# Attention's values on two column tiles, sums of probabilities on GpSimd, maxima written straight into the queries

## The reference, cut to what matters

```
s = (einsum("bqhd,bkhd->bhqk", q_nope, k_nope) + einsum("bqhr,bkr->bhqk", q_rope, k_rope)) * SM_SCALE
s = where(allowed, s, finfo(float32).min)
p = softmax(s, axis=-1)
out = einsum("bhqk,bkhd->bqhd", p, v)
```

## Time and profile before

| | us |
|---|---|
| median of three runs | 1343.7 (1342.97 to 1345.61) |
| the profiled execution, its own time | 1344.39 |
| span of its instructions | 1342.6 |
| PE busy in it | 1312.1 (98%) |
| DVE, ACT, POOL busy | 891.2, 502.8, 57.3 |
| the eight heads of attention | 434.0 to 587.3 |

### The profile page before, as it was taken

One profiled execution on the slowest core, in us unless ns is written; L12 is line 12 of the kernel. 1 busy time (PEld: TensorE's weight loads), 2 busy tenths in 40 slices (PEclk: granted clock), 3 DMA queues, 4 the chain that ended last, 5 costly groups with the idle time before them and its releaser, 6 DMA issues.

```text
span 1342.6 us, 22926 instructions
## 1 busy us (share of the span) xinstructions
PE 1312.1 (98%) x9288; PEld 1245.7 (93%) x9288; DVE 891.2 (66%) x1391; ACT 502.8 (37%) x833; POOL 57.3 (4%) x59
## 2 busy tenths in 40 slices
PE   6999999999999999999999999999999999999997
PEld 4799999999997677789999999999999999999997
DVE  6699988382655567777885545656456569877743
ACT  5622221234301444346643333333333336444532
POOL 0200000000013122200000000000000000000000
PEclk9899999999999999999999999999999999999999
DMA  9445534711213332030232232331323276455441
GB/s 352 142 142 149 160 116 114 279 37 31 91 30 68 110 78 45 1 100 13 68 101 88 63 110 97 119 103 58 108 88 119 88 275 235 118 178 160 163 138 79
DMA packets 132759, 154.75 MB, mean 115 GB/s; under 512 B 12065, under 2 KB 99705, under 8 KB 130641
## 3 DMA queue, kind: packets, MB, share of 16 engines
q1 hardware_dynamic: 130080, 152.50, 35.8%
q10 hardware_dynamic: 2608, 1.28, 0.4%
HBM read 115.51 MB, written 30.69 MB: 109 GB/s over the span
## 4 chain that ended last, share of the span: by engine, by line
PE 91%; DVE 5%; ACT 1%; issue 1%; DMA 1%; POOL 0%; SPq 0%; ACTq 0%; DVEq 0%; POOLq 0%
PE PS L1360 30%; PE PS L917 18%; PE PS L1426 12%; PE PS L1456 5%; PE PS L1270 4%; PE PS L1123 4%; PE PS L1503 3%; PE PS L1250 3%; PE PS L1308 2%; PE PS L1011 2%; PE PS L1197 2%; PE PS L1217 1%; PE PS L1151 1%; DVE MX L2432 1%; PE PS L886 1%
## 5 line engine op out<-in xcount | busy, mean ns | idle before, releaser
L1360 PE MATMUL PS<-HBL_T,EH 128*128 128x264 f32 x640 | 169.3, 285 | 0.0
L1360 PE MATMUL PS<-HBH_T,EH 128*128 128x264 f32 x640 | 169.1, 284 | 0.0
L917 PE MATMUL PS<-HH,WH 128*128 128x352 f32 x432 | 139.7, 324 | 1.6 <-DVE CQ L2299 0.8
L917 PE MATMUL PS<-HL,WH 128*128 128x352 f32 x432 | 139.0, 323 | 0.0
L1360 PE MATMUL PS<-HBH_T,EL 128*128 128x264 f32 x640 | 130.4, 285 | 0.0
L1360 PE MATMUL PS<-HBL_B,EH 128*128 128x264 f32 x480 | 127.5, 286 | 0.0
L1360 PE MATMUL PS<-HBH_B,EH 128*128 128x264 f32 x480 | 127.1, 285 | 0.0
L1360 PEld LDWEIGHTS PS<-HBH_T,EH 128*128 128x128 f32 x640 | 120.6, 188 | 0.0
L1360 PEld LDWEIGHTS PS<-HBL_T,EH 128*128 128x128 f32 x640 | 120.3, 188 | 0.0
L1426 PE MATMUL PS<-DTH,DWH 128*128 128x264 f32 x440 | 116.6, 286 | 0.1
L1426 PE MATMUL PS<-DTL,DWH 128*128 128x264 f32 x440 | 116.7, 285 | 0.0
(11 more groups left out here) (346 smaller groups left out, 3166.4 us busy)
## 6 DMA issues: line engine op xcount, KB each, us to landing
ADA<-in_w_ada SPq DMA_DIRECT2D x22, 1024.0 KB, 6.0
DTR<-saved_operands SPq DMA_DIRECT2D x66, 264.0 KB, 2.9
HALF_W<-in_w_gate SPq DMA_DIRECT2D x22, 512.0 KB, 4.0
saved_operands<-UP SPq DMA_DIRECT2D x10, 1056.0 KB, 4.0
RAW<-in_w_in SPq DMA_DIRECT2D x20, 512.0 KB, 6.6
DWR<-in_w_down SPq DMA_DIRECT2D x33, 256.0 KB, 3.2
HALF_W<-in_w_up SPq DMA_DIRECT2D x12, 512.0 KB, 3.7
saved_operands<-TB SPq DMA_DIRECT2D x11, 528.0 KB, 4.8
```

Source lines behind the costliest of these rows:

```text
L917: mm = pe.matmul(PS[:, b + n, 0:CH], w, x[k][:, n * CH:(n + 1) * CH], start=(first and w is weights[0][k] and x is xs[0]), stop=(last and ...
L1360: mm = pe.matmul(PS[:, 2 * s + n, 0:HQ], w, x[:, k, n * HQ:(n + 1) * HQ], start=(first and w is wh and x is xh), stop=(ends and w is wl), ...
```

## The change

Four edits, all in attention:

- `values(h, i)` has 64 stationary columns (the values alone) and becomes two matmuls: the query tiles of even number go to one column tile of PE (PSUM partitions 0 to 63 or 64 to 127), the odd ones to the other; `tile_half` says which. All eight query tiles now fit into bank 4.
- The probabilities of step 0 go to `ACC0`, one buffer per head in turn; `add_probabilities` (POOL) adds those of steps 1 to 7 to it, and `sums(h)` multiplies the total once with the ones, again on two column tiles, in step 0 of the next head (for the last head behind step 8). An exponential waits for the addition two steps back too.
- The maxima go by the same two transfers into `QTH` directly; `MROW` is float32r, so that DVE's copy rounds. `QTM`, `round_maxima` and `max_rounded` are gone; `scores(h, 0)` waits for the transfers.
- `keep_output` copies the values after step 8, the sample's after the next exponential, the sums one step later; `invert_last_sums` waits for all of it.

```diff
+        def row_tiles(ap, first):
+            return ap.rearrange("p (t c) -> p t c", c=P)[:, first::2, :]
+        def tile_half(h, parity):
+            e = (h + parity) % 2
+            return slice(VH * e, VH * (e + 1))
...
 def load_maxima(h):
                 sp.wait_ge(m_kept, h + 1)
-                if h >= 1:
-                    sp.wait_ge(max_rounded, h)
-                sp.dma_start(QTM[PLAIN:CONTRACT, 0:S]..., MROW[0:KD, h % 2, :]).then_inc(max_rows, 16)
-                sp.dma_start(QTM[PLAIN:CONTRACT, S:T], MROW[KD:KD + 1, h % 2, 0:SD]).then_inc(max_rows, 16)
+                if h >= 2:
+                    sp.wait_ge(s_full, STEPS * (h - 1))
+                sp.wait_ge(rounded, 2 * h + 1)
+                row = QTH[h % 2][PLAIN:CONTRACT, :].bitcast(F32)
+                (the same two transfers into row)
...
 def scores(h, i): (i == 0)
-                    pe.wait_ge(max_rounded, h + 1)
+                    pe.wait_ge(max_rows, 32 * (h + 1))
...
 def values(h, i): (i < KD)
-                    for bank, lo, hi, stop in ((4, q0, 512, 3), (5, max(q0, 512), S, KD - 1)):
-                        if lo < hi:
-                            mm = pe.matmul(PS[:, bank, ...], V[:, i, h // 2, VH * (h % 2):VH * (h % 2) + P], PP[...])
+                    for parity in ((0, 1), (1, 0))[i % 2]:
+                        t = i + (i + parity) % 2
+                        if t < KD:
+                            mm = pe.matmul(PS[tile_half(h, parity), 4, P * (t // 2):512], V[:, i, j, P * e:P * e + VH],
+                                           row_tiles(probabilities(h, i), t - i), ...)
+            def sums(h):
+                pe.wait_ge(p_added, (KD - 1) * (h + 1))
+                pe.wait_ge(o_kept, 3 * h + 2)
+                for parity in range(2):
+                    mm = pe.matmul(PS[tile_half(h, parity), 5, :], V[:, 0, 0, VH:2 * VH], row_tiles(ACC0[:, h % 2, :], parity), ...)
...
                         score_maxima(h + 1, (i, 0))
+                    if i == 0 and h >= 1:
+                        sums(h - 1)
                     values(h, i)
...
+            sums(HEADS - 1)
...
 def exponentials(h, i): (0 < i < KD, but for i == 2)
+                    act.wait_ge(p_used, (KD - 1) * h + (i - 1 if i > 1 else 0))
+                    act.wait_ge(p_added, (KD - 1) * h + i - 2)
...
+            def add_probabilities(h, i):
+                n = (KD - 1) * h + i - 1
+                if i == 1:
+                    pool.wait_ge(p_used, n + 1)
+                pool.wait_ge(exp_done, STEPS * h + i + 1)
+                if n >= 1:
+                    pool.wait_ge(p_added, n)
+                pool.tensor_tensor(ACC0[:, h % 2, P * i:], ACC0[:, h % 2, P * i:], PP[:, n % 2, 0:S - P * i], ALU.add)\
+                    .then_inc(p_added, 1)
...
-            round_maxima(0)
-            for h in range(1, HEADS):
-                round_maxima(h)
-                if h + 1 < HEADS:
+            for h in range(HEADS):
+                if 1 <= h < HEADS - 1:
                     round_head(h + 1)
+                for i in range(1, KD):
+                    add_probabilities(h, i)
```

More of the change, by code:

```diff
@@ L1258, in scores, with probabilities @@
                 mm.then_inc(s_full, 1)
+            def probabilities(h, i):
+                return ACC0[:, h % 2, :] if i == 0 else PP[:, (7 * h + i - 1) % 2, 0:S - P * i]
             def values(h, i):
-                n = STEPS * h + i
-                pe.wait_ge(exp_done, n + 1)
+                j, e = divmod(h, 2)
+                pe.wait_ge(exp_done, STEPS * h + i + 1)
                 if i < KD:
-                    q0 = P * i
                     if i == 0 and h >= 1:
-                        pe.wait_ge(o_kept, 3 * h)
-                    for bank, lo, hi, stop in ((4, q0, 512, 3), (5, max(q0, 512), S, KD - 1)):
-                        if lo < hi:
[L1270 to L1277, removed]
+                        pe.wait_ge(o_kept, 3 * h - 2)
+                    for parity in ((0, 1), (1, 0))[i % 2]:
+                        t = i + (i + parity) % 2
+                        if t < KD:
+                            mm = pe.matmul(PS[tile_half(h, parity), 4, P * (t // 2):512], V[:, i, j, P * e:P * e + VH],
+                                           row_tiles(probabilities(h, i), t - i), start=(i == 0), stop=(i == KD - 2 + parity))
+                    mm.then_inc(p_used if i < KD - 1 else o_full, 1)
+                else:
+                    if h >= 1:
+                        pe.wait_ge(o_kept, 3 * h)
@@ L1278, in values @@
                     for m in range(3):
                         _, r = key_tile(KD + m)
[L1280 to L1281 removed]
+                        mm = pe.matmul(PS[:, 5, 0:SD], V[0:r, KD + m, j, VH * e:VH * e + P],
+                                       PSM[0:r, (STEPS * h + i) % 2, SD * m:SD * (m + 1)], start=(m == 0), stop=(m == 2))
@@ L1282, in values @@
                     mm.then_inc(o_full, 1)
+            def sums(h):
+                pe.wait_ge(p_added, (KD - 1) * (h + 1))
+                pe.wait_ge(o_kept, 3 * h + 2)
+                for parity in range(2):
+                    mm = pe.matmul(PS[tile_half(h, parity), 5, :], V[:, 0, 0, VH:2 * VH], row_tiles(ACC0[:, h % 2, :], parity),
+                                   start=True, stop=True)
+                mm.then_inc(o_full, 1)
             pe.wait_ge(ones_kept, 1)
@@ L1750, in exponentials @@
                 act.wait_ge(s_full, n + 1)
-                if i == 0 and h >= 1:
+                if i == 0 and h >= 2:
+                    act.wait_ge(o_full, 3 * h - 3)
+                elif i == 2 and h >= 1:
+                    act.wait_ge(o_full, 3 * h - 2)
+                    act.wait_ge(p_added, (KD - 1) * h)
+                elif 0 < i < KD and (KD - 1) * h + i >= 3:
+                    act.wait_ge(p_used, (KD - 1) * h + (i - 1 if i > 1 else 0))
+                    act.wait_ge(p_added, (KD - 1) * h + i - 2)
+                elif i == KD and h >= 1:
                     act.wait_ge(o_full, 3 * h - 1)
[L1753 to L1756, removed]
                 if i < KD:
                     nq = S - P * i
-                    act.activation(PP[:, n % 2, 0:nq], PS[:, b:b + 2, :].rearrange("p b q -> p (b q)")[:, 0:nq], ACT.Exp,
+                    dst = ACC0[:, h % 2, :] if i == 0 else PP[:, ((KD - 1) * h + i - 1) % 2, 0:nq]
+                    act.activation(dst, PS[:, b:b + 2, :].rearrange("p b q -> p (b q)")[:, 0:nq], ACT.Exp,
                                    scale=SCALE).then_inc(exp_done, 1)
@@ L1774, in keep_output @@
                     act.wait_ge(ao_lo, j - 1)
-                act.activation(OP[j % 2][rows, t], src[rows, :], ACT.Copy)
-                act.activation(SUMS[j % 2][rows, t], src[VH * (1 - e):VH * (2 - e), :], ACT.Copy).then_inc(o_kept, 1)
+                if part == 1:
+                    act.activation(OP[j % 2][rows, S:T], PS[rows, 5, 0:SD], ACT.Copy)
+                    ins = act.activation(SUMS[j % 2][rows, S:T], PS[VH * (1 - e):VH * (2 - e), 5, 0:SD], ACT.Copy)
+                else:
+                    dst, bank = ((OP[j % 2], 4), None, (SUMS[j % 2], 5))[part]
+                    for parity in range(2):
+                        ins = act.activation(row_tiles(dst[rows, 0:S], parity),
+                                             PS[tile_half(h, parity), bank, :].rearrange("p (t c) -> p t c", c=P), ACT.Copy)
+                ins.then_inc(o_kept, 1)
             def round_ao(m):
@@ L1784, in _ @@
             for h in range(HEADS):
-                for i in range(1, 5):
+                for i in range(1, STEPS):
                     exponentials(h, i)
[L1787 to L1790, removed]
+                    if i == 1 and h >= 1:
+                        keep_output(h - 1, 2)
+                    if h == HEADS - 1 and 5 <= i < STEPS - 1:
                         if i == 5:
```

32 lines of the change are left out of this document (11 added, 21 removed).

## The result

The kernel after took **1370.4 us** (median of 4 runs, 1366.85 to 1383.75), the kernel before 1344.2 on the same chip: ratio 1.0216, 95% interval 1.019 to 1.0241. It is slower, as forecast, but by 26 us and not by 12, and the time lies above the range (1342.5 to 1366). Whether it is slower by more than 2% the interval leaves open. The profiled execution took 1371.47 us, its span is 1369.4, 26.8 above the span of before. The mean granted clock of the four runs is 0.984, 0.980, 0.982 and 0.969 for 1366.85, 1369.34, 1371.47 and 1383.75 us: the fastest has the highest and the slowest the lowest.

A forecast was written before the change was run, and what follows sets the result against it. PE, busy for 98% of the span, was taken as the bound. PE's account +0.8, maxima -0.5, POOL against DVE +11.6 and tail +0.2 made +12.1 us on 1343.7: 1356 us, range 1342.5 to 1366.

The forecast's parts named there:

- The account of PE: PE in attention: column tiles save 3.44 us a head, sums add 0.86, switches 2.8; +0.1 a head counted, 0.8 in all.
- The rival that the switch costs nothing: PE's switches between tilings cost nothing with 64 columns and additions stay hidden: 12.8 us saved, 1331 us; chance 0.10.
- the one that the tiles don't run at once: PE's column tiles run one after another, so each head pays sums and switches extra: 1380 us; chance 0.04.
- The maxima: POOL's rounding of the maxima goes; it hid under PE but for 0.5 us, so -0.5 us.
- The additions' own length: POOL's additions take 2.3 ns a column; 3584 columns make 8.2 us, 9.3 with seven waits.
- POOL against DVE: At heads' ends, whichever engine comes second waits for the first's whole instruction, so PE waits: +11.6 us, bounds 0 and 20.
- its marks: Attention: ACT waits for additions, PE for ACT; KTL 2.5 us or more; first maxima product waits for POOL, heads 3 and 5.
- the rival that the casts come late in all heads: DVE wins each contest and POOL's casts come late in all six heads, 1.3 us more each: 1364 us; chance 0.12.
- The sum: Whole kernel: 0.8 - 0.5 + 11.6 + 0.2 (tail) = +12.1 us, added to the median 1343.7: 1356 us.

The follow-up runs named there:

- e10: e9 with the values of steps 4 and 5, and of 6 and 7, next to each other on PE; 1345.84 us, ratio 1.0009 to the kernel before.
- e3: The kernel after without POOL's additions and their waits, the sums replaced by 1; 1344.44 us, ratio 1.0005 to the kernel before.
- e1: The kernel before with only the maxima going directly into the queries; 1342.45 us, ratio 0.9986 to the kernel before.
- e11: The kernel after with DVE made to wait for the additions of steps 4, 5 and 6 before KTL, OP by SUMS and AOH; 1363.67 us.
- e12: e7 with two useless exponentials in step 6 in place of three; 1371.25 us, ratio 1.0194 to the kernel before.
- e7: e1 with three useless exponentials on ACT in each head's step 6, as a delay; 1395.92 us, ratio 1.0381 to the kernel before.
- e8: e3 with the same delay of three useless exponentials on ACT as e7; 1396.26 us, ratio 1.0395 to the kernel before.
- e2: e1 with POOL's additions and their waits, values and sums still full-width as before; 1359.02 us, ratio 1.0116 to the kernel before.
- e4: The kernel after with four buffers for the probabilities instead of two; 1358.25 us, ratio 1.0118 to the kernel before.
- e5: e4 with POOL's casts for a head moved ahead of the additions of steps 5 to 7; 1353.19 us, ratio 1.0067 to the kernel before.
- e6: e5 with the values of neighbouring steps in pairs, 0 and 1 through 6 and 7; 1362.82 us, ratio 1.0142 to the kernel before.
- e9: e5 with a head's sums moved on PE from step 0 to step 3 of the next head; 1349.27 us, ratio 1.0035 to the kernel before.

## Why the prediction was right or wrong

**The account of PE** (+0.8) was right. The tiles overlap, a switch costs 0.34 (0.32 by e10) where 0.35 was taken, and e3 stands 0.16 a head above e1 where 0.1 was forecast. The rival that the switch costs nothing fell, and so did the one that the tiles don't run at once.

**The maxima** (-0.5) gained 1.9 us (0.5 to 3.1 by the interval), 0.2 a head.

**The additions' own length** was right: 2.3 ns a column was taken, 2115 ns for 896 columns is 2.36.

**POOL against DVE** (+11.6) was right in kind. Two of its marks are there: ACT's line 1786 waits for additions, PE for ACT. Two are not. KTL stays at 1.51 us in heads 2 to 6 (the forecast said 2.5 or more; heads 0 and 1 have 2.22). And no maxima product waits for a cast in heads 3 and 5, for which 2.0 us each were counted: their loss stands at exponential 7, as one wait of 2.06 and 2.04 us where 0.9 was forecast. So the rival that the casts come late in all heads (1364 us) fell too. Waits and all else, without the clock, come to 26.8 - 18.7 = 8.1 us, of which 1.1 lie ahead of attention (its first product starts at 435.18, at 434.12 before). By head it was less well placed: heads 0 to 3, all at a clock of 1.00, lost 4.0 together (19.03, 20.58, 20.37 and 21.55 against 19.40, 19.51, 19.23 and 19.37), where 5.8 was forecast for them. One assumption in it was wrong: that one addition runs between each two of DVE's instructions. DVE's went three in a row, and the addition of step 4 took 3.38 us on average, up to 4.61, not 2.3. By e11, which forces the assumed order, this costs 6.7 us, and that is clock: 37.4 us low became 20.5, worth 8.5. PE's idle times of 0.3 us and more in attention add up to 9.2 us in e11 and 9.1 in after, since the casts now came late.

The Trainium skill, "SBUF — State Buffer", section "SBUF: two separate sides", says of a GpSimd operation and a VectorE one that has two SBUF inputs or runs in a two-port mode that whichever starts first gets the port pair for the whole instruction, and the other blocks. The trace agrees for one instruction of each (the cast AOH at 513.40 took 1.66 us, not 0.71, with an addition in its way). When DVE had a second instruction ready while the addition waited, DVE went first here, at 510.69 and at 512.12.

**The sum is the step that failed.** It added PE's waits at their own length. A term for the clock was missing: 37.4 us at 1.2 GHz, 18.7 us, more than all of PE's idle time in attention together (9.1 us). With it, 12.1 + 18.7 = 31 would have been too high by 4; with the waits as measured it is 26.8. e12 shows the term by itself, where a wait of 1.5 us a head and nothing else brings 37.7 us at the lower level, and e7 and e8 show that it is there with tiles and without. The profile of before could have warned of it: attention ran at 1.00 with PE idle for 0.2 us of a head, so the rows held no case of a wait of over 1 us in attention, and I took the absence of such a case for a price of nothing. The forecast's range had no case with a clock below 1.00 either, and that is why it was too narrow above.

**What stays open.** e2 has PE's waits of after (6.5 and 6.8 us) and 10.3 us low, not 37.4; e4 has 10.2. Waits of 0.8 to 0.9 us were followed by low stretches in after (541.2, 589.0 and 612.9) and by none in e2; waits of 1.63 us (e5), 1.51 (two of e12's), 2.45 (e4) and 2.37 (e6, at 545.6) by none; and two stretches begin in waits of only 0.5 to 0.7 us (e11 at 580.5, e3 at 585.5). Which waits bring the clock down is thus not settled by their length alone, and nor is why after has so much more of it than e2. That TensorE is busier between them in e2 (values of full width) fits, but e7 and e8 differ in the same way, and there the tiles made only 7 us of low clock more. An experiment with DVE's low parts made short, to take the contest away and keep the additions, was not tried: QTL and KTL are written in the place of QT and KT.

## What to carry to other kernels

Where TensorE is busy for 98% of a stretch at the full clock, a wait put into it is not priced at its length: here a wait of 1.5 or 2.6 us in every head (e12, e7) cost two to three times that, so an edit that saves TensorE nothing and puts an engine in front of it can only lose. An engine that is free by its share (POOL is busy for 106.5 of 183 us here) has no room where VectorE runs three instructions in a row beside it, and each wait that was taken away (buffers, then casts, then sums) uncovered the next in the same row of work. Before narrowing matmuls, count the switches: at 0.34 us for in and out, eight a head take 2.7 of the 3.4 us saved, and the sums' 0.86 the rest.

## What the runs showed of the hardware

- TensorE in column tiles with plain float32: two tiles of 64 columns run at once; 2 x 512 columns in 0.96 us, where one tile of 128 took 1.72 for the 1024.
- Going into the tiles and back to 128 columns costs 0.34 us (e3) or 0.32 (e10 against e9); three products per step that stay outside them are enough to pay it each time.
- GpSimd's addition of 512 columns took 4.61 us with three of VectorE's two-input instructions back to back ahead of it, 2.27 with one (e11).
- The clock fell from 2.4 to 1.2 GHz behind waits of 0.8 to 2.6 us of an otherwise busy TensorE (after, e12, e7), and stayed low for 3.4 to 10.2 us each time. It did so behind all eight waits of 2.57 us (e7), six of eight of 1.51 (e12) and neither of two of 1.63 (e5). In e9, where the longest idle time of PE is 0.81 us (from 589.1), one stretch of 3.4 us was left, at 589.9.
